# An attention stage on one core: the causal mask added in PSUM by a TensorE product, queries scaled as they leave PSUM, the last value banks reordered

## The reference

```
q = (rms_norm(c_q, q_norm) @ w_uq).reshape(B, S, MLA_HEADS, NOPE_DIM + ROPE_DIM)
q_rope = apply_rope(q[..., NOPE_DIM:], cos, sin)
...
s = (jnp.einsum('bhqd,bhkd->bhqk', qn_b, kn)
     + jnp.einsum('bhqr,bkr->bhqk', qr_b, k_rope))
s = s.astype(jnp.float32) * scale                 # scale = 96 ** -0.5
s = jnp.where(key_idx[None, :] <= q_idx[:, None], s, neg)
p = jax.nn.softmax(s, axis=-1)
return jnp.einsum('bhqk,bhkd->bhqd', p.astype(vh.dtype), vh)
```

## Time and profile before

| | us |
|---|---|
| Median of 3 runs | 1550.77 |
| Lowest and highest | 1547.91, 1551.12 |
| The profiled execution's own time | 1551.75 |
| Its span from first to last instruction | 1549.2 |
| The attention stage in it (first scores to last transposition) | 111.7 to 266.0 |

### The profile page before, as it was taken

The page is one execution under the profiler, slowest core; times in us unless marked ns, Lnnn a source line. Parts: engine busy times, 40 slices in busy tenths (PEclk is TensorE's granted clock), DMA queues, the critical chain, the costliest instruction groups (busy, mean ns, idle before and its releaser), DMA issues.

```text
span 1549.2 us, 26173 instructions
## 1 busy us (share of the span) xinstructions
PE 1505.4 (97%) x10293; PEld 1215.7 (78%) x10293; DVE 1079.8 (70%) x1776; ACT 659.2 (43%) x1165; POOL 98.5 (6%) x181
## 2 busy tenths in 40 slices
PE   6999999999999999999999999999999999999998
PEld 5976666787777887888787887888888888887876
DVE  6468986467787581577866469777777747877786
ACT  7544454344433212445423236444444533433453
POOL 1010000000010001255100020000000000000000
PEclk9999999999999999999999999999999999999999
DMA  5030000713222535302357213444444689878754
GB/s 195 14 78 28 1 1 3 203 41 106 65 69 65 161 129 131 103 4 68 114 162 261 75 55 129 151 151 153 155 155 146 215 307 326 298 279 279 272 188 150
DMA packets 176752, 212.41 MB, mean 137 GB/s; under 512 B 28645, under 2 KB 110946, under 8 KB 176002
## 3 DMA queue, kind: packets, MB, share of 16 engines
q1 hardware_dynamic: 176574, 210.91, 41.1%
q10 hardware_dynamic: 68, 0.02, 0.0%
HBM read 154.11 MB, written 54.82 MB: 135 GB/s over the span
## 4 chain that ended last, share of the span: by engine, by line
PE 67%; DVE 16%; DMA 10%; issue 3%; SPq 2%; ACT 2%; POOL 0%; DVEq 0%; ACTq 0%; POOLq 0%
PE bank L3255 19%; PE bank L2856 11%; DMA down_raw<-in_w_ff_down 7%; PE bank L3167 5%; PE bank L3220 5%; PE bank L3319 5%; PE bank L2756 3%; PE bank L2716 2%; PE bank L2649 2%; PE bank L2769 2%; PE bank L2784 2%; DVE xprod L2067 2%; DVE mg_lo L2483 2%; DVE mg_hi L2481 2%; PE bank L2794 1%
## 5 line engine op out<-in xcount | busy, mean ns | idle before, releaser
L2856 PE MATMUL bank<-uT_hi,w_hi 128*128 128x512 f32 x432 | 171.3, 396 | 0.0
L2856 PE MATMUL bank<-uT_hi,w_lo 128*128 128x512 f32 x432 | 168.2, 389 | 0.0
L2856 PE MATMUL bank<-uT_lo,w_hi 128*128 128x512 f32 x432 | 168.2, 389 | 0.0
L3319 PE MATMUL bank<-mg_lo,mg_hi 128*128 128x512 f32 x576 | 135.2, 390 | 2.1 <-DVE mg_lo L2483 1.9
L3319 PEld LDWEIGHTS bank<-mg_lo,mg_hi 128*128 128x128 f32 x576 | 107.7, 188 | 26.3 <-DVE mg_lo L2483 4.0
L3319 PE MATMUL bank<-yh,mg_lo 128*128 128x512 f32 x384 | 118.7, 390 | 0.5 <-DVE yl L2483 0.4
L1260 ACT ACTIVATE zbuf<-bank 128x512 f32<-128x512 f32 x54 | 32.4, 599 | 181.7 <-PE bank L2856 177.7
L2856 PEld LDWEIGHTS bank<-uT_hi,w_hi 128*128 128x128 f32 x432 | 81.1, 188 | 21.9 <-issue 5.2
L1607 ACT ACTIVATE f<-f 128x512 f32<-128x512 f32 x64 | 40.5, 632 | 131.6 <-DVE f L2435 69.6
L2856 PEld LDWEIGHTS bank<-uT_hi,w_lo 128*128 128x128 f32 x432 | 81.1, 188 | 17.3 <-issue 1.0
L2856 PEld LDWEIGHTS bank<-uT_lo,w_hi 128*128 128x128 f32 x432 | 81.1, 188 | 17.0
(11 more groups left out here) (498 smaller groups left out, 3772.7 us busy)
## 6 DMA issues: line engine op xcount, KB each, us to landing
down_raw<-in_w_ff_down SPq DMA_DIRECT2D x80, 512.0 KB, 5.4
down_raw<-f_spill SPq DMA_DIRECT2D x56, 512.0 KB, 4.0
f_spill<-x SPq DMA_DIRECT2D x80, 256.0 KB, 2.6
w_raw<-in_w_in SPq DMA_DIRECT2D x28, 512.0 KB, 4.1
sgate<-gate_spill SPq DMA_DIRECT2D x16, 512.0 KB, 4.3
up_a<-in_w_ff_up SPq DMA_DIRECT2D x16, 512.0 KB, 4.7
up_b<-in_w_ff_up SPq DMA_DIRECT2D x16, 512.0 KB, 4.2
f_spill<-f SPq DMA_DIRECT2D x32, 256.0 KB, 2.3
```

What stands on the lines that cost most here:

```text
L2856: ins = nc.tensor.matmul(ps[2 * slot + g][:], st[:, slot, k, :], mv[:, k, g * HALF:(g + 1) * HALF], start=(k == 0 and m == 0), stop=(k == ...
L3319: ins = nc.tensor.matmul(ps[4 * (q % 2) + t][:], st, mv_, start=(start and w == 0 and m == 0), stop=(stop and w == 1 and m == 2))
```

## The change

- The mask is no longer added by DVE. POOL makes a copy of the identity in fp32r (`identr`) and an fp32r mask matrix with -2^127. After the products of a unit's scores PE adds identity x mask onto the 128 diagonal columns in PSUM, without clearing them, and this product now announces the scores.
- The queries are multiplied with the softmax scale when they leave PSUM: on ACT as the copy's scale, on DVE in the rotary multiplications and in a multiplication instead of a copy. The exponential then has no scale, and DVE's scaling of the maximum goes.
- The eight last projections, the values, go to banks in the order 2, 6, 7, 0, 4, 1, 5, 3. Waits are for the last user of the same bank (`last_out`). The first scores wait only for bank 0; the waits for the last evacuations come after the second scores, ahead of unit 0 and unit 1.

```diff
-NEG = -3.0e38
+NEG = -2.0 ** 127
...
-BANKS = (2, 6, 7, 4, 5, 3, 0, 1)
+BANKS = 3 * (2, 6, 7, 4, 5, 3, 0, 1) + (2, 6, 7, 0, 4, 1, 5, 3)
+def last_out(bank, n=len(OUTS)):
+    return max(m for m in range(n) if BANKS[m] == bank)
...
-                pch(pool, nc.gpsimd.memset(cneg[:], 0.0))
-                nc.gpsimd.affine_select(out=cneg[:], in_=cneg[:], compare_op=ALU.is_ge, fill=NEG, base=0,
+                pool.wait_ge(s_const, 2)
+                pch(pool, nc.gpsimd.tensor_scalar(identr[:], ident[:], 1.0, 0.0, ALU.mult, ALU.add))
+                pch(pool, nc.gpsimd.tensor_scalar(cneg[:], ident[:], 0.0, 0.0, ALU.mult, ALU.add))
+                nc.gpsimd.affine_select(out=cneg[:], in_=cneg[:].bitcast(F32), compare_op=ALU.is_ge, fill=NEG, base=0,
                                         pattern=[[-1, P]], channel_multiplier=1).then_inc(s_cst2, 1)
...
-                                             ps[BANKS[n % 8]][0:NOPE, :], ACT.Copy).then_inc(s_qa, 1)
+                                             ps[BANKS[n]][0:NOPE, :], ACT.Copy,
+                                             scale=SM_SCALE if kind == "q" else 1.0).then_inc(s_qa, 1)
...
-                    nc.scalar.activation(pexp[:, u % 2, 0:n0], ps[b0][:, 0:n0], ACT.Exp, bias=sc, scale=SM_SCALE,
+                    nc.scalar.activation(pexp[:, u % 2, 0:n0], ps[b0][:, 0:n0], ACT.Exp, bias=sc,
...
-                        nc.vector.tensor_tensor(rp_cos[:], bank[:], cosT[:, sl], ALU.mult).then_inc(s_qd, 1)
+                        nc.vector.scalar_tensor_tensor(rp_cos[:], bank[:], SM_SCALE, cosT[:, sl], ALU.mult, ALU.mult).then_inc(s_qd, 1)
...
+                    elif kind == "q":
+                        nc.vector.tensor_scalar(qT[0:NOPE, 2 * j + 1, sl], bank[NOPE:P, :], SM_SCALE, None, ALU.mult).then_inc(s_qd, 1)
...
                 def row_max(u):
...
-                    if u == 0:
-                        dve.wait_ge(s_cst2, 1)
...
-                    db = ps[b0 + i // 4][:, (i % 4) * P:(i % 4 + 1) * P]
-                    dch(dve, nc.vector.tensor_tensor(db, db, cneg[:], ALU.add))
...
-                        dch(dve, nc.vector.tensor_reduce(small[:, m:m + 1], ps[b0][:, 0:n], AXX, ALU.max, negate=True))
+                        nc.vector.tensor_reduce(sc, ps[b0][:, 0:n], AXX, ALU.max, negate=True).then_inc(s_mx, 1)
...
-                        dch(dve, nc.vector.tensor_tensor(small[:, m:m + 1], small[:, m + 1:m + 2], small[:, m + 2:m + 3], ALU.min))
-                    nc.vector.tensor_scalar(small[:, 192 + u % 2:193 + u % 2], small[:, m:m + 1], SM_SCALE, None,
-                                            ALU.mult).then_inc(s_mx, 1)
+                        nc.vector.tensor_tensor(sc, small[:, m + 1:m + 2], small[:, m + 2:m + 3], ALU.min).then_inc(s_mx, 1)
...
-                        pe.wait_ge(s_qa, evacuated_act(n - 8))
-                        pe.wait_ge(s_qd, evacuated_dve(n - 8))
+                        pe.wait_ge(s_qa, evacuated_act(last_out(BANKS[n], n)))
+                        pe.wait_ge(s_qd, evacuated_dve(last_out(BANKS[n], n)))
...
-                        ins = nc.tensor.matmul(ps[b0 + g][:, 0:w], qT[0:QH, h, i * P:(i + 1) * P],
-                                               kT[0:QH, h, 512 * g:512 * g + w], start=True, stop=True)
-                    ins.then_inc(s_sc, 1)
+                        nc.tensor.matmul(ps[b0 + g][:, 0:w], qT[0:QH, h, i * P:(i + 1) * P],
+                                         kT[0:QH, h, 512 * g:512 * g + w], start=True, stop=True)
+                    nc.tensor.matmul(ps[b0 + i // 4][:, (i % 4) * P:(i % 4 + 1) * P], identr[:], cneg[:],
+                                     start=False, stop=True, skip_group_check=True).then_inc(s_sc, 1)
...
-                pe.wait_ge(s_qa, evacuated_act(len(OUTS) - 1))
-                pe.wait_ge(s_qd, evacuated_dve(len(OUTS) - 1))
+                pe.wait_ge(s_qa, evacuated_act(last_out(0)))
+                pe.wait_ge(s_qd, evacuated_dve(last_out(0)))
                 pe.wait_ge(s_rd, 16 * (1 + 16))
+                pe.wait_ge(s_cst2, 1)
                 scores(0)
                 for u in range(NT * NH):
                     if u + 1 < NT * NH:
                         scores(u + 1)
+                    if u < 2:
+                        n = last_out((1, 3)[u])
+                        pe.wait_ge(s_qa, evacuated_act(n))
+                        pe.wait_ge(s_qd, evacuated_dve(n))
```

More of the change, by code:

```diff
@@ L259, in program @@
             0, ("ident", [P, P], F32), ("vcol", [P, 64], F32), ("vrow", [P, P], F32), ("bones", [P, P], F32),
-            ("small", [P, 256], F32), ("cneg", [P, P], F32), ("cmask", [P, 2, 256], F32),
+            ("small", [P, 256], F32), ("cneg", [P, P], F32R), ("cmask", [P, 2, 256], F32),
             ("cosv", [P, NT, 16], F32), ("sinv", [P, NT, 16], F32),
@@ L265, in program @@
         rsum = kr[:].rearrange("p i r -> p (i r)")
-        assert top["ident"] <= 11
+        identr, = place(10.5, ("identr", [P, P], F32R))
+        assert top["ident"] <= 10.5
         uT = place(11, ("uT_hi", [P, KD, T], F32R), ("uT_lo", [P, KD, T], F32R))
@@ L1189, in _ @@
                         nc.scalar.activation((qT if kind == "q" else kT)[0:NOPE, 2 * j, g * HALF:(g + 1) * HALF],
-                                             ps[BANKS[n % 8]][0:NOPE, :], ACT.Copy).then_inc(s_qa, 1)
+                                             ps[BANKS[n]][0:NOPE, :], ACT.Copy,
+                                             scale=SM_SCALE if kind == "q" else 1.0).then_inc(s_qa, 1)
                     elif kind == "v" and j % 2 == 0:
                         act.wait_ge(s_qp, n + 1)
-                        nc.scalar.activation(vm[:, j, :], ps[BANKS[n % 8]][:], ACT.Copy).then_inc(s_qa, 1)
+                        nc.scalar.activation(vm[:, j, :], ps[BANKS[n]][:], ACT.Copy).then_inc(s_qa, 1)
                 def round_fill(n):
@@ L1220, in _ @@
                     n0 = min(n, 512)
-                    nc.scalar.activation(pexp[:, u % 2, 0:n0], ps[b0][:, 0:n0], ACT.Exp, bias=sc, scale=SM_SCALE,
+                    nc.scalar.activation(pexp[:, u % 2, 0:n0], ps[b0][:, 0:n0], ACT.Exp, bias=sc,
                                          accum_out=psums[:, 0, u:u + 1]).then_inc(s_ex, 1)
                     if n > 512:
-                        nc.scalar.activation(pexp[:, u % 2, 512:n], ps[b0 + 1][:, 0:n - 512], ACT.Exp, bias=sc, scale=SM_SCALE,
+                        nc.scalar.activation(pexp[:, u % 2, 512:n], ps[b0 + 1][:, 0:n - 512], ACT.Exp, bias=sc,
                                              accum_out=psums[:, 1, u:u + 1]).then_inc(s_ex, 1)
@@ L1871, in _ @@
                 for n, (kind, g, j) in enumerate(OUTS):
[L1872 removed]
+                    sl, bank = slice(g * HALF, (g + 1) * HALF), ps[BANKS[n]]
                     if kind == "v" and j % 2 == 0:
@@ L1895, in row_max @@
                     b0, n = 2 * (u % 2), (i + 1) * P
-                    db = ps[b0 + i // 4][:, (i % 4) * P:(i % 4 + 1) * P]
-                    dch(dve, nc.vector.tensor_tensor(db, db, cneg[:], ALU.add))
-                    m = 160 + 4 * (u % 2)
+                    m, sc = 160 + 4 * (u % 2), small[:, 192 + u % 2:193 + u % 2]
                     if n <= 512:
-                        dch(dve, nc.vector.tensor_reduce(small[:, m:m + 1], ps[b0][:, 0:n], AXX, ALU.max, negate=True))
+                        nc.vector.tensor_reduce(sc, ps[b0][:, 0:n], AXX, ALU.max, negate=True).then_inc(s_mx, 1)
                     else:
```

6 lines of the change are left out of this document (3 added, 3 removed).

## The result

| | before | after |
|---|---|---|
| Median | 1548.99 (17 runs) | 1553.91 (17 runs) |
| Lowest and highest | 1545.38, 1551.12 | 1547.44, 1557.67 |
| The profiled execution's own time | 1551.75 | 1553.91 |
| Its span | 1549.2 | 1552.2 |

The ratio is 1.0029, with an interval of [1.0018, 1.0040]. The forecast was 1551.0 and "the same"; the range, 1547.5 to 1558.5, holds the result. But the kernel before is itself 1.8 us lower in these 17 runs than in the three that the forecast started from. The difference is +4.9 us where +0.2 was forecast, and by the prediction's own mark of 0.2% that is slower and not the same.

A forecast was written before the change was run, and what follows sets the result against it. TensorE was taken as the bound nearly everywhere. Mask products at +6.65 us less 6.43 us given back made +0.2 us on a median of 1550.77: 1551.0 us, "the same", range 1547.5 to 1558.5.

The forecast's parts named there:

- The stalls: Attention stage: TensorE's waits for transpositions and at start and end shrink, giving 6.43 us back together.
- The 0.40 at the start: Start of the attention: TensorE's 0.40 us wait before the first transposition goes.
- C: Rival: ScalarE's own exponentials and copies hold the transpositions, so the stalls stay; +5.9 us, 1556.7 us; chance 0.05.
- A: Rival: the short fp32r mask product runs at fp32 pace, 0.22 us each; +6.8 us, 1557.6 us; chance 0.34.
- The banks: Start of the attention: first scores begin 0.99 us sooner, worth nothing because the first fill product waits for `fw_lo`.
- the scaling of the queries: Projections: eight VectorE multiplications become three-operand ones, 0.06 us more each, costing nothing while TensorE still projects.
- 0.61 foreseen: VectorE in the attention: without the scaling, the copy follows the maximum after about 0.61 us.
- 61 x 0.109 = 6.65 us more: TensorE in the attention: 61 mask products on its path, each priced at the pace of a transposition.
- rival B: The mask product costs only its columns, 0.06 us, its weight load hidden; -2.8 us, 1548.0 us; chance 0.23.
- My own sign of being wrong: Undisturbed last blocks: the 7.02 us per two units grows by 0.12 or 0.44 us instead of 0.22.
- B's doubt about short scores: Against the 0.06 us price: blocks 0 and 1 have only short scores records to hide the load under.
- No DMA is added or moved. All later loads hang on TensorE's progress and shift with it.: Stages behind the attention: loads only shift with TensorE; no cost was counted.

The follow-up runs named there:

- 2: Also written `scale_only`: the kernel before with only the softmax scaling moved to the queries, mask and banks unchanged; 1546.31 us, ratio 0.9987.
- 7: Also written `scale_banks`: the kernel before with query scaling and the new bank order, mask left on VectorE; 1546.81 us, ratio 0.9989.
- experiment 6: The changed kernel with the mask product made twice per unit, each with half the mask value; 1553.46 us, ratio 1.0032 to the kernel before.
- changed_pad64: The changed kernel with 64 small transpositions added in TensorE's first wait; 1546.73 us, ratio 0.9985 to the kernel before.
- lower group: The five kernels whose TensorE instruction packets stand half a packet off from the kernel before; store wait 6.04 to 6.07 us against 4.67 to 4.71.
- as_changed: The changed kernel timed again with no edit, beside the kernel before; 1553.65 us, ratio 1.0032.
- padded kernels: Kernels with 32, 64 or 128 small transpositions added to TensorE's first wait; ratios to the kernel before from 0.9985 to 1.0042.
- same_before: The kernel before timed again against itself with no edit; 1550.08 us, ratio 1.0012.
- mask_only: The kernel before with only the mask product moved to TensorE, VectorE still scaling the maximum, banks unchanged; 1554.86 us, ratio 1.0046.
- before_pad64: The kernel before with 64 small transpositions added in TensorE's first wait, no other change; 1556.86 us, ratio 1.0042.

## Why the prediction was right and wrong

**Right.** The stalls: summed over the stage they give about 6.4 us back, 6.43 foreseen. The 0.40 at the start is gone. C is excluded by the waits of PE, and A by the price of the product. The banks are worth nothing since `fw_lo` covers them, and the scaling of the queries costs nothing in the projections (2 and 7). It even costs less than I took, 0.06 us for each of the eight three-operand multiplications: they take 688 and 683 ns, the two-operand ones of before 688 and 682. VectorE's copy follows the maximum after 0.60 us, 0.61 foreseen: **the timeline of DVE after**

```profile
154.64 0.68 DVE L1908 TENSOR_REDUCE small<-bank 128x1 f32<-128x512 f32 x1
155.24 0.68 DVE L1920 COPY pT<-bank 128x512 f32<-128x512 f32 x1
```

**Mis-sized: "61 x 0.109 = 6.65 us more".** The product costs 0.061 us in most places and 0.11 ahead of a gate product: some 53 x 0.061 + 8 x 0.11 = 4.1 us. 4.1 - 6.4 gives -2.3, and the stretch 0-263 shows -2.4. That is rival B's size, and its 0.06 us had stood among my bounds: I chose between them by likeness to the transposition, where the place decides. My own sign of being wrong came true: the pace of two units grew by 0.11 us, B's 0.12 and not the forecast's 0.22. B's doubt about short scores was not the right one either. Behind scores of one block the product costs 0.062 ahead of values and 0.11 ahead of a gate product, so there what follows it makes the difference; and directly behind another mask product it costs 0.112 (experiment 6). The Trainium skill, "TensorE: Matmul & The Clock Gate", has both numbers: its section on the back-to-back issue gap gives about 56 ns for 128 columns, for a product taken by itself, and the section on LDWEIGHTS about 107 ns. The trace agrees with each in one kind of place (61 ns, and 110 to 112 ns). The first section also gives about 81 ns for a stream of weight loads and products of 128 columns, and no place here shows that. That a weight load, hidden or not, is what separates the two prices is argued and not shown: no run changed the load alone.

**Failed: "No DMA is added or moved. All later loads hang on TensorE's progress and shift with it."** Half a packet more in TensorE's instruction stream made every kernel slower behind the attention, with the mask product or without it. The last column of the first table gives 4.7 to 7.7 us for the five kernels concerned, against -0.8 to +1.9 for the others; for the changed kernel it is 7.3, which turned a gain of 2.4 us in the stage into +4.9. The sum had this term at nothing, and its price of the product was 2.5 us too high. That the result lies inside the stated range is luck: the range was made wide by rival A, whose price of 0.22 us the trace rules out, and the term that filled it is in none of the rivals. The range of the likeliest case alone, 1548.5 to 1552.5, does not hold it.

**Against the parts.** The scaling alone gives 3.2 us for nothing. With it in place, the mask product adds some 4.1 and so gives back 3.2: the stretch is 259.74 in `scale_banks` and 260.63 in after, one execution each at a clock of 1.00. So here it is a small loss in the stage even without the packets, though the whole kernels that would show it, `scale_banks` and `changed_pad64`, cannot be told apart (0.9989 and 0.9985). The scaling alone, or the changed kernel with the 64 transpositions, beats both kernels (0.9987 and 0.9985); the two cannot be told apart.

**Open.** That the packet delays the store inside the DMA engines is read from its place in thirteen traces; I did not see how. Of some 7 us, this store's wait is 1.37. That TensorE waits for its instructions near 615 and 650 us is not shown, and neither is what ties the wait for `hn` to the packets. Why the granted clock falls more often in the lower group is open too: the same instructions ran through 346-352 at 1.00 in after and at 0.81 in `as_changed`. The clock does account for two things that the stretches show. All the padded kernels but `changed_pad64` are 1.4 to 1.8 us slower within 0-263 than the kernels they are made from, and `as_changed` is 1.6 us slower there than after; these five have a clock of 0.94 between 100 and 130 us, all others 1.00. Whether the padding brings this fall about is not shown, as `as_changed` has none. The stretch 700-712 takes 12.0 us in before, `same_before` and `scale_only`, at 0.86, and 10.5 in all others, at 1.00. The stretches were chosen after looking at after and `mask_only`; `before_pad64` and `changed_pad64` were run to test the choice.

## What to carry to other kernels

Price a small product by its place, with the products directly ahead of it and behind it, and not by one number for all places: the same product cost 0.06 us ahead of values and transpositions and 0.11 ahead of a gate product or behind its own twin. When a change of under 1% adds or removes some hundred instructions, compare the untouched stages product by product with the granted clock of each stretch beside them, and run a control that adds the same number of harmless instructions to the kernel before; without it, a layout effect is taken for the change's own worth. Where a change has two halves, time each alone: here the free half gave a larger gain in the stage (3.2 us) than the two together (2.4).

## What was not expected of the hardware

- 64 transpositions in an idle time of TensorE made the kernel before 0.42% slower, and 128 of them did not (1.0009). 64 made the changed kernel faster by about 0.45% (from 1.0029 or 1.0032 to 0.9985).
- One 16 KB instruction packet of 0.92 us, starting 2.4 us after the issue of a store of 512 KB, goes with 1.37 us more until that store has landed.
- The mean granted clock over all runs is 0.9961 to 0.9966 in the five kernels whose packets stand half a packet off, and 0.9975 to 0.9983 in the others.
- Behind the longer wait the granted clock went to 0.50 for some microseconds in some executions (`as_changed`) and stayed at 1.00 in others (after), with the same instructions.
